# Moving the summing columns behind the large arrays in a one-core diffusion-trunk kernel

## What is computed

```python
def pre_norm(x, mod, j, g):
    return rmsnorm(x, g) * (1 + mod_chunk(mod, 3 * j + 1)) + mod_chunk(mod, 3 * j)

def post_residual(x, out, mod, j, g, w):
    return x + w * mod_chunk(mod, 3 * j + 2) * rmsnorm(out, g)

def swiglu(h, w_in, w_out):
    gate, up = jnp.split(h @ w_in, 2, axis=-1)
    return (jax.nn.silu(gate) * up) @ w_out
```

## Time and profile before

| what | us |
|---|---|
| median of 3 runs | 1701.79 |
| lowest and highest | 1696.65, 1702.23 |
| the profiled execution's own time | 1699.4 |
| its span, first to last instruction | 1697.6 |
| PE busy | 1639.4 |
| PEld busy | 1592.4 |
| DVE busy | 840.9 |
| ACT busy | 694.7 |
| POOL busy | 30.3 |
| mean granted TensorE clock | 0.987 |

### The profile page before, as it was taken

The page is one execution under the profiler, slowest core; times in us unless marked ns, Lnnn a source line. Parts: engine busy times, 40 slices in busy tenths (PEclk is TensorE's granted clock), DMA queues, the critical chain, the costliest instruction groups (busy, mean ns, idle before and its releaser), DMA issues.

```text
span 1697.6 us, 27632 instructions
## 1 busy us (share of the span) xinstructions
PE 1639.4 (97%) x11325; PEld 1592.4 (94%) x11325; DVE 840.9 (50%) x1328; ACT 694.7 (41%) x1205; POOL 30.3 (2%) x41
## 2 busy tenths in 40 slices
PE   5999999999998989999999999999999989999997
PEld 4999999998887988999999899999999989999997
DVE  5544434463447896443435734333562867344333
ACT  3433333353543465333334533333453346333332
POOL 2000000002100000000000000000000000000000
PEclk9999999999998998999999999999999999999999
DMA  9633366658981134433334533336453455443311
GB/s 329 221 124 124 124 211 218 218 187 253 283 280 50 56 115 149 142 124 124 113 128 155 174 125 124 124 118 205 149 174 125 141 182 175 129 132 125 114 44 38
DMA packets 255668, 259.91 MB, mean 153 GB/s; under 512 B 6625, under 2 KB 253826, under 8 KB 255570
## 3 DMA queue, kind: packets, MB, share of 16 engines
q1 hardware_dynamic: 249664, 251.67, 45.8%
q10 hardware_dynamic: 4978, 4.41, 0.8%
q0 software_dynamic: 928, 2.44, 0.6%
HBM read 255.88 MB, written 2.62 MB: 152 GB/s over the span
## 4 chain that ended last, share of the span: by engine, by line
PE 87%; DVE 7%; ACT 2%; issue 2%; POOL 1%; DMA 0%; ACTq 0%; DVEq 0%; POOLq 0%
PE bank L441 24%; PE bank L443 24%; PE bank L442 24%; PE bank L1487 3%; PE bank L466 1%; PE bank L1531 1%; PE bank L471 1%; PE bank L467 1%; DVE WL L407 1%; DVE X L1082 1%; PE bank L1767 1%; ACT WH L394 1%; PE bank L1538 1%; DVE SUMS L1338 1%; POOL WL L407 1%
## 5 line engine op out<-in xcount | busy, mean ns | idle before, releaser
L407 DVE TENSOR_TENSOR WL<-RAW,WH 128x1024 fp32r<-128x1024 f32 x330 | 394.9, 1199 | 698.1 <-ACT WH L394 697.3
L394 ACT ACTIVATE WH<-RAW 128x1024 fp32r<-128x1024 f32 (+1 forms) x334 | 346.5, 1044 | 656.6 <-PE bank L443 645.8
L441 PE MATMUL bank<-HH,WH 128*128 128x384 f32 x1664 | 566.2, 340 | 6.7 <-DVE WL L407 4.1
L443 PE MATMUL bank<-HH,WL 128*128 128x384 f32 x1664 | 562.9, 338 | 0.0
L442 PE MATMUL bank<-HL,WH 128*128 128x384 f32 x1664 | 562.7, 338 | 0.0
L441 PEld LDWEIGHTS bank<-HH,WH 128*128 128x128 f32 x1664 | 313.5, 188 | 9.7 <-DVE WL L407 4.6
L442 PEld LDWEIGHTS bank<-HL,WH 128*128 128x128 f32 x1664 | 313.5, 188 | 0.0
L443 PEld LDWEIGHTS bank<-HH,WL 128*128 128x128 f32 x1664 | 313.2, 188 | 0.0
L441 PE MATMUL bank<-AH,WH 128*128 128x384 f32 x704 | 238.4, 339 | 0.0
L442 PE MATMUL bank<-AL,WH 128*128 128x384 f32 x704 | 236.8, 336 | 0.0
L443 PE MATMUL bank<-AH,WL 128*128 128x384 f32 x704 | 236.7, 336 | 0.0
(11 more groups left out here) (227 smaller groups left out, 1444.5 us busy)
## 6 DMA issues: line engine op xcount, KB each, us to landing
RAW<-in_ffn_w_in SPq DMA_DIRECT2D x88, 1024.0 KB, 5.1
RAW<-in_mod_w SPq DMA_DIRECT2D x72, 1024.0 KB, 6.6
RAW<-in_ffn_w_out SPq DMA_DIRECT2D x32, 1024.0 KB, 5.2
RAW<-in_ab_w_in SPq DMA_DIRECT2D x16, 1024.0 KB, 8.5
RAW<-in_ffn_w_out SPq DMA_DIRECT2D x16, 768.0 KB, 4.6
RAW<-in_cv_w_in SPq DMA_DIRECT2D x12, 1024.0 KB, 5.2
RAW<-in_ab_w_out SPq DMA_DIRECT2D x4, 1024.0 KB, 8.9
RAW<-in_cv_w_out SPq DMA_DIRECT2D x4, 1024.0 KB, 6.0
```

The costliest lines, as they stand in the source:

```text
L394: e.activation(w_high(st, 2 * jj + b)[:, 0:nk, :], RAW[:, p, 0:nk, b * P:(b + 1) * P], ACT.Copy).then_inc(half_hi, 1)
L407: e.tensor_tensor(w_low(st, 2 * jj + b)[:, 0:nk, :], RAW[:, p, 0:nk, b * P:(b + 1) * P], w_high(st, 2 * jj + b)[:, 0:nk, :].bitcast(F32), ...
L441: e.matmul(out, hi[:, kk, :], xh(kk), start=(first and kk == 0), stop=False)
L443: mm = e.matmul(out, lo[:, kk, :], xh(kk), start=False, stop=(last and kk == nk - 1))
```

## The change

The declaration of W7 moves from its place ahead of EPSC to the end, behind MIX. EPSC becomes the first column of an array of 16 columns. The name EPSC is that one column as before, so its readers are as before.

```diff
@@ -190,8 +190,7 @@
         LBT = sb("LBT", [P, 4, 8])
         SMALL = sb("SMALL", [P, 3, 4])
         STAT = sb("STAT", [P, 8, TOKS])
-        W7 = sb("W7", [P, 2, 2, SUM_COLS])
-        EPSC = sb("EPSC", [P, 1])
+        EPSC = sb("EPSC", [P, 16])[:, 0:1]
 
         with nc.sbuf_tensor("OUTF", [P, KD, NT], F32) as OUTF:
             pass
@@ -219,6 +218,7 @@
 
         LEAD = {at: lead(at) for at in sorted({at for s in LEAD_AT for at in LEAD_AT[s]})}
         MIX = sb("MIX", [P, MIX_WORDS])
+        W7 = sb("W7", [P, 2, 2, SUM_COLS])
 
         def mix(at, *shape):
             n = int(np.prod(shape))
```

## The result

| | before | after |
|---|---|---|
| median of 7 runs, us | 1697.28 | 1684.34 |
| lowest to highest | 1696.65 to 1702.23 | 1682.62 to 1690.28 |
| profiled execution, its span | 1699.4, 1697.6 | 1683.63, 1681.8 |
| mean granted TensorE clock in it | 0.987 | 0.987 |

The ratio is 0.992, with a 95% interval of 0.9903 to 0.9937. The kernel got faster by 0.8%, and 1684.34 lies outside the stated range of 1692 to 1708. It is the end that rival 2 gave (1686.5), to which I had given 6 in 100. The forecast started from three runs and the profiled one; the seven runs of the kernel before have the median 1697.28, so 2.7 of the 15.7 us between forecast and result lie in the starting point and not in the change.

What follows compares the result with a forecast made beforehand. The prediction took PE's 7872 matmuls with 384 moving columns, about 1382 of 1697.6 us, to bound the kernel. Every term of the change was 0, so it forecast 1700.0 us, the mean of three runs and the profiled one, range 1692 to 1708.

Steps and rivals of the forecast that it cites:

- rival 2: PE's large matmuls: the new address favours the low level, removing 12.9 us, time 1686.5; chance 6%.
- PE's moving operands: HH, HL, AH, AL moving 736 bytes to 32 beyond a multiple of 64: between +27.6 and -12.9 us, taken as 0.
- W7's row: L1531's matmul, moving operand 32 beyond a multiple of 64: median 275 ns, same as for ONES, read as no surcharge.
- the pace is unmoved by all that does vary: PE's matmuls: 17 starts in 3 us with transfers at 329 or 9 GB/s, a reason for taking 0.
- Addresses alone therefore do not choose the level: Sublayer 5 at 173.3 ns, sublayers 0, 2, 3 and 4 at 176.8, same arrays: something other than addresses chooses.
- Meetings of engines in the memory: PE's reads delayed when DVE, ACT or a transfer touches the memory: bounded to some ns a matmul, taken as 0.
- lines of 16 bytes: Memory read rule for moved arrays: 736 bytes is 46 whole lines, so the sum stays at 0.
- ACT and DVE: Their reads and writes of moved arrays: a 40-byte offset costs at most 1 ns in 550, cost 0.
- my own sign: Prediction wrong if an ACT or DVE group on MIX, HH or AH changes its mean more than its neighbour on SQ or TT.
- W7, EPSC, transfers: W7 and EPSC keep their place within 64 bytes, cost 0; loads and stores touching MIX 0, with +-1 us kept.
- Rival 3: PE's stretches fall on different levels by chance, without link to the address: 1692 or 1706; beyond 5.1 us, 6% each way.
- Rival 1: Every matmul with 384 moving columns: the 32-byte offset costs PE a step, +27.6 us if on all, 1727; chance 6%.

Runs made afterwards that it cites:

- e3: Kernel before with 32 bytes of padding ahead of X, so every array stands 32 bytes higher; ratio to before 1.0013, median 1698.93 us.
- e4: Kernel before with 32 bytes ahead of WH and 32 behind WL, HH and all behind 64 bytes higher; ratio to before 0.992, median 1683.86 us.
- w_d96: Kernel before with only WH and WL moved against HH and AH, 96 bytes ahead and 160 behind; ratio to before 1.0071, median 1706.95 us.
- w_d224: Kernel before with only WH and WL moved against HH and AH, 224 bytes ahead and 32 behind; ratio to before 0.9904, median 1686.02 us.
- e1: Kernel before with EPSC as 16 columns and W7 left in place, HH and all behind it 32 bytes up; ratio to before 0.9931, median 1690.04 us.
- e2: Changed kernel with EPSC as 24 columns, HH and all behind it 32 bytes higher; ratio to kernel before 0.9925, median 1688.99 us.
- e10: Kernel before with STAT behind MIX, EPSC 8 columns, W7 and 96 bytes between HL and MIX, moving HH and HL; ratio 1.0027, median 1704.74 us.
- e6: Kernel before with W7 between HL and MIX and EPSC at 40 columns, moving HH and AH; ratio to before 0.9899, median 1684.58 us.
- w_d64: Kernel before with only WH and WL moved against HH and AH, 128 bytes ahead and 128 behind; ratio 0.9942, median 1684.76 us.

## Why the prediction was wrong

**The bound** was right: PE's matmuls with 384 moving columns, 7872 of them, at two levels, 173.3 and 176.8 ns, both at full granted clock. What can be assigned of the change's effect, 14.1 of 15.8 us, lies there.

**The step that failed** is "PE's moving operands ... I take 0". The range for it was right on the side that came true: 12.9 us for taking the slow level away where it stood, which is what the long stretches gave back. That they agree to the tenth says only that the new level is the old low one, since the matmuls are the same. Three reasons drove the choice of 0 between the ends, and all were weak. The first was W7's row, durations of a matmul whose pace I could not see; a latency says nothing of a pace, as L441's own 340 and 339 ns now show. The second was that "the pace is unmoved by all that does vary": what varied in those rows was transfers and vector work, not the distance of two addresses. The third was "Addresses alone therefore do not choose the level", since the low level stood in sublayer 5 with the same arrays. That was a reading of one execution as if the levels were fixed to the sublayers. The second profile of the same kernel has the low level in the HH stretches of sublayers 0, 2, 3 and 5 and the high one in 4. At D = 192 the addresses leave both levels open; at other distances they decide: always low in the profiles at 224, 0 and 64, always above it at 96 and 128. Both readings fit the first profile, and the forecast used only one.

**The question was put for the wrong address.** I weighed HH's place within 64 bytes, that is, one array by itself. e3 and e4 show that a distance between two arrays counts, WH to HH, and that WH need not be touched by the diff for it to change. "Meetings of engines in the memory" was the right kind of thought, but I looked for another engine at the other end. DVE, ACT and transfers are not needed to hold a level: both stand where PE works alone (w_d96 and the changed kernel above). What is left are two streams of PE's own, weights and moving columns. The earlier trace rows compared stretches in which these two were alike, so it could not show them. I also read the earlier trace rows wrongly there: "DVE busy 41 to 46% at either level" holds for the high level, and the low one had 39% and the least traffic. The conclusion stood by luck, until the second profile bore it out.

The Trainium skill's lines of 16 bytes (SBUF — State Buffer, door 1, the box on "cachelines") gave 0 for a move of 46 whole lines; the measured 0.8% disagrees, so that rule is not the whole of what an address costs. From the figures of the Trainium skill (TensorE: Matmul & The Clock Gate, "Wait — 56ns, not 53.3ns?") I had estimated the distance at 162.5 ns; the best of any kernel here is 173.3, so the disagreement that I took as a hint remains at every D.

**ACT and DVE:** 0 was right; 736 bytes changed their means by 0 to 3 ns of 607. By the letter of my own sign the 3 ns of L699 on MIX are more than the 2 ns of its neighbour on SQ; that is 1 ns in 600, and in sublayer 1 it is the other way round. **W7, EPSC, transfers:** 0 was right; the wait for x to land is 2.1 us as before, and w_d224 gives the whole gain with W7 at its old place, e1 too.

**Rival 2** had the mechanism's outward form and the price, 1686.5 against 1684.34, and was dismissed with the false inference above. **Rival 3** was right that levels fall differently from one execution to the next. That is part of why runs of the kernel before spread from 1689 to 1709; the 41 runs of kernels whose profile has no slow stretch still spread by 8.4 us, and there the time goes with the granted clock. Rival 1, a step up on each matmul, did not occur here, but w_d96 is such a case, at D = 96, and costs 0.7%, since before has part of its stretches at the high level already. As D could have landed on 96 or 128 as well as on 224, a fair forecast without these runs would have given each side far more than 12%.

**Left open.** That the two reads of PE delay each other in the memory is an inference: the runs show that the distance of their addresses decides, that nothing else tried does and that a level holds with no other engine at work, not what happens at the meeting. Why 32 is mixed between 0 and 64, why 96 and 128 are slow in every stretch, and what sets the level of a stretch at D = 192, they do not tell. All but the kernel before have one profile each, so "always" rests on the stretches of one or two kernels and on the times of their runs. That the measure is 256 bytes rests on pairs 256 apart that agree (192 and 448, 64 and 320, 128 and 384, 224 and 480). No version beats the changed kernel: D = 0 and 64 give the same pace and medians of 1684.6 to 1689.0. That e1 and e2 have higher medians than the changed kernel at the same pace goes with the granted clock: e1's five runs are 1682.96 and 1683.06 us at a mean clock of 0.989 and 1690.04 to 1690.18 at 0.983.

## What to carry to other kernels

Where back-to-back matmuls bound a kernel, note the addresses of the stationary and the moving array modulo 256, and count starts per microsecond in a clean stretch; 2% of pace (173.3 against 176.7 ns) hung on their distance here. Which distances are good is shown for these matmuls alone, 128x128 float32 weights and 384 moving columns. Any declaration that grows ahead of one of the two changes it, so a kernel that got slower by "nothing" after a buffer was enlarged should be tried with 32 to 64 bytes of padding before the enlargement is blamed; from D = 192 both were enough, but from D = 64 the same step would lead to a slow one. Take two profiles of one kernel before calling a level a property of a place in the program.

## What the runs showed that I had not expected

- The pace of a matmul with 384 moving columns has locked levels at one granted clock. By the start times they are 173.3, 174.7, 175.6, 176.0 and 176.7 ns. They hold for hundreds of matmuls and change after a break, or, in e10, at the matmul where the moving array changes to one at another D.
- With D = 128 the start times of the records repeat a pattern of five, 182, 176, 173, 174 and 175 ns, in most stretches, whichever of the three products it falls on.
- At D = 192 the same kernel on one chip spreads by 1% (31 runs, 1689.63 to 1706.32 us). At D = 64 the six runs of e6 lie within 2.3 us (1684.43 to 1686.67) and those of w_d64 within 8.4 (1682.70 to 1691.05). So the chance levels are only part of the spread, and the granted clock is another.
